# Two gated chunks in the plain form instead of four, twenty from seven products, in the second feed-forward layer

## The chip, the cores and the metric

The kernel runs on one core of a Trainium2 chip. The metric is the device time of one execution in microseconds (us), from the first instruction to the last with what the launch adds around them; lower is better.

## The reference, cut to what matters

A decoder trunk of two layers over 1024 tokens of width 1024: a Conformer convolution layer, then a differential-attention layer, each followed by a SwiGLU feed-forward layer with 2816 hidden units, and a last RMSNorm. The change touches only the second feed-forward layer:

```python
def swiglu(h, w1, w3, w2):
    return (jax.nn.silu(h @ w1) * (h @ w3)) @ w2

x = x + swiglu(rmsnorm(x, ffn_norm_g[layer]), ffn_w1[layer], ffn_w3[layer], ffn_w2[layer])
```

## The kernel before, in words

All activations stand transposed: 128 channels on the partitions, 1024 tokens in two halves LA and LB of 512. Every float32 product is made from three fp32r matmuls: each operand is split into a high part (a rounded copy, made by ScalarE) and a low part (the difference, made by VectorE), and high by low, low by high and high by high are added up in PSUM. The function `product` issues these three; one of them has a 128x128 weight tile and 512 columns.

The 2816 hidden units are 22 chunks of 128. For the gated part of the second layer (`silu(h @ w1) * (h @ w3)`) there are two forms.

**The plain form.** `F1` holds its plan; its `sizes` say how many chunks are made so. A chunk has two blocks, one of w1 and one of w3. A block is 8 chunks of the contraction, 3 matmuls and 2 halves: 48 matmuls, issued by `both` (line 2160), and the last block by `dense` (lines 2022 to 2024). Blocks are numbered i = 0, 1, ... On each block VectorE and ScalarE do, in order: split the weights of block i + 2 (`hi`, line 923; `lo`, line 1367), then what the function `beside_f1(i)` holds, then the evacuation. A w1 block is evacuated by a multiplication with `rstd` (line 1561, semaphore `t1_ok`) and a Silu (line 1049); a w3 block by two VectorE operations for each half (lines 1572 and 1575, `t3_ok` and `g_ok`). The gated rows go to DRAM (`hidden_store`).

**Seven products (Winograd's form of Strassen's method).** The other chunks are taken in pairs. A unit is one matrix (w1 or w3) for a pair of chunks: the weights and the operand are each four quarters, and seven products (`A11, S2, A12, S1, S3, S4, A22`) of sums of quarters replace eight. A product is 4 chunks of the contraction and 3 matmuls: 12 matmuls, so a unit is 84. `UNITS = FC - CHUNKS0`, which is 18 units for the 18 chunks. The sums of the operand's quarters are made once, before the first unit, by this chain:

- ScalarE `sum_parts` (line 1274, 8 copies) makes `tv`; VectorE `sums_first` (lines 1834 and 1837, 4 + 4 operations) and `sums_last` (lines 1843 and 1846, 4 + 4) make the sums in `tv`.
- ScalarE `sum_high` (line 1281) makes the high part of a sum, VectorE `sum_low(n, turn)` (line 1853) its low part, 4 operations each for each of the sums 1, 3, 2 and at last 0. Sum 0 lies over an operand of the plain form, and so its `sum_high` waits until the last plain block is done.
- For unit 0, the weights' sums: `weight_sums_first` and `weight_sums_last` (lines 1877 to 1887, 4 operations), and the splits of six products' weights, `up_high` (line 1297) and `up_low` (line 1862). The seventh, `A22`, comes after the last plain block.

All of these VectorE operations have 512 columns. In the kernel before they stand beside blocks 2 to 7, as the diff shows. TensorE waits before each product for that product's `up_low` (`u_lo`), in unit 0 also for the `sum_low` of its operand, and for the PSUM bank. Every engine works through its instructions strictly in the order written.

The weights of unit 0 are loaded by `up_load(0)`, which SyncE issues behind the `hidden_store` of an earlier chunk and after the last `lo`; `up_load(u + 1)` waits for all seven `up_low` of unit u. Behind the last unit the down projection begins (`STEPS_D` steps in three parts of tokens); `DOWN_ORDER` names the order in which part 0 uses the banks, which follows from the bank of the last product.

Of the kernel before, what the change touches and what calls it, by code (L numbers as in the profile page):

```python
# [18 lines left out]
KC = D // P  # L19
TB = T // P  # L20
F = 2816
FC = F // P
# [13 lines left out]
LA, LB = 0, 1  # L36
# [64 lines left out]
F0B = Ffn(0, (LB,), (8, 7, 7), PW2B + KC, F0A.result0 + F0A.results() + KC, FC, 0, 3 * KC, False)  # L101
ATT0 = F0B.block0 + F0B.blocks()
WO0 = ATT0 + 3 * HEADS
F1 = Ffn(1, (LA, LB), (4,), WO0 + KC + 1, F0B.result0 + F0B.results(), 2 * FC, FC, 6 * KC, False, True)
TAIL = F1.block0 + F1.blocks()
BLOCKS = TAIL

CHUNKS0 = F1.sizes[0]  # L110
UNITS = FC - CHUNKS0
# [9 lines left out]


PARTS = ((0, HT), (HT, HT // 2), (HT + HT // 2, HT // 2))
DOWN_ORDER = ((2, 3, 6, 7, 4, 5, 0, 1), tuple(range(KC)), tuple(range(KC)))
DOWN_BANK = (tuple((n, 0) for n in range(KC)), tuple(((2, 3, 6, 7)[n // 2], n % 2 * HT // 2) for n in range(KC)),
             tuple(((4, 5, 0, 1)[n // 2], n % 2 * HT // 2) for n in range(KC)))
STEPS_D = len(PARTS) * FC
# [36 lines left out]
def results_through(b):  # L164
# [9 lines left out]
    if b < ATT0:  # L174
        return F0B.result0 + b - F0B.block0 + 1
    return F1.result0 + 2 * (b - F1.block0 + 1)

# [184 lines left out]
def trunk(nc, a, out):  # L362
    with ExitStack() as ctx:
# [5 lines left out]
        def sem(name):  # L369
            return ctx.enter_context(nc.semaphore(name))  # L370
# [157 lines left out]
        t1_ok = sem("t1_ok")  # L528
        t3_ok = sem("t3_ok")
# [86 lines left out]
        def down_size(b):  # L616

            for f in (F0A, F0B, F1):
                if f.block0 <= b < f.block0 + f.blocks():
# [24 lines left out]
        def _(sp):  # L644
# [19 lines left out]
            def cols(w, n):  # L664
                return w[:, :, n * P:(n + 1) * P]
# [20 lines left out]

            up1 = w1[F1.layer].rearrange("(k p) n -> p k n", p=P)
            up3 = w3[F1.layer].rearrange("(k p) n -> p k n", p=P)
            down = w2[F1.layer].rearrange("(k p) (n c) -> k p n c", p=P, c=P)
# [45 lines left out]
            def second_layer():  # L735
                blocks = list(F1.order())
                for _, what, c, b in blocks[0:4]:
                    load(b, cols(up1 if what == "w1" else up3, c))
                for i in range(len(blocks)):
                    if i + 4 < len(blocks):  # L740
                        _, what, c, b = blocks[i + 4]
                        load(b, cols(up1 if what == "w1" else up3, c))
                    if i == 6:
                        up_load(0)
                    if i % 2:
                        hidden_store(i // 2)
                for u in range(UNITS):
                    if u + 1 < UNITS:
                        up_load(u + 1)
                    else:  # L750
                        down_load(0)
                        down_load(1)
                    if u % 2:
                        for j in range(4):
                            if u == UNITS - 1 and j == 3:
                                down_load(2)
                                down_load(3)
                            unit_store(u, j)
                            if u == UNITS - 1 and j < 2:
                                hidden_load(2 * j)  # L760
                                hidden_load(2 * j + 1)
                for d in range(4, STEPS_D):
                    down_load(d)
                    hidden_load(d)
                    if d == 8:
                        for j in range(4):
                            sp.wait_ge(g_out[j], 16 * (UNITS // 2))
                        sp.dma_start(grow[:, :], a["final_norm_g"].unsqueeze(0).broadcast_to([P, D])) \
                            .then_inc(grow_in, 16)
                    t = y_behind(d - 8)  # L770
                    if t is not None:
                        y_store(t)
# [111 lines left out]
        def _(act):  # L884
# [385 lines left out]
            def sum_parts():  # L1270

                for k in range(HC):
                    for to, hf in ((tv[1], LA), (tv[2], LB)):
                        act.activation(by_block(to[:, k, :]), X(k, hf), ACT.Copy,
                                       scale=col("ffn_norm_g", KC + k)).then_inc(t_e, 1)
# [25 lines left out]
                act.activation(st[:, j, :], st[:, j, :], ACT.Silu).then_inc(u_silu, 1)  # L1301

            def beside_f1(i):
                if i == 2:
                    sum_parts()
                if i == 4:
                    sum_high(1, HC)
                if i == 5:
                    sum_high(3, 2 * HC)
                    sum_high(2, 3 * HC)  # L1310
                if i == 7:
                    for j in range(A22):
                        up_high(0, j)

# [45 lines left out]
        def _(dve):  # L1360
# [469 lines left out]
            def sums_first():  # L1830

                for k in range(HC):
                    dve.wait_ge(t_e, 2 * k + 2)
                    dve.tensor_tensor(tv[0][:, k, :], tv[2][:, k, :], tv[1][:, k, :], ALU.subtract).then_inc(t_v, 1)
                for k in range(HC):
                    dve.wait_ge(t_v, k + 1)
                    dve.scalar_tensor_tensor(by_block(tv[1][:, k, :]), X(HC + k, LB), col("ffn_norm_g", KC + HC + k),
                                             by_block(tv[0][:, k, :]), ALU.mult, ALU.subtract).then_inc(t_v, 1)

            def sums_last():  # L1840
                for k in range(HC):
                    dve.wait_ge(t_v, HC + k + 1)
                    dve.scalar_tensor_tensor(by_block(tv[3][:, k, :]), X(HC + k, LA), col("ffn_norm_g", KC + HC + k),
                                             by_block(tv[1][:, k, :]), ALU.mult, ALU.subtract).then_inc(t_v, 1)
                for k in range(HC):
                    dve.scalar_tensor_tensor(by_block(tv[2][:, k, :]), X(HC + k, LB), col("ffn_norm_g", KC + HC + k),
                                             by_block(tv[2][:, k, :]), ALU.mult, ALU.subtract).then_inc(t_v, 1)

            def sum_low(n, turn):

                for k in range(HC):
                    dve.wait_ge(t_hi, HC * turn + k + 1)
                    dve.tensor_tensor(Tl[n][:, k, :], tv[n][:, k, :], Th[n][:, k, :].bitcast(F32),
                                      ALU.subtract).then_inc(t_lo, 1)
# [32 lines left out]
                dve.tensor_tensor(s4, raw[0][:, HC:KC, :], s2v[:, :, :], ALU.subtract).then_inc(u_sum, 1)  # L1887

            def beside_f1(i):
                if i == 3:  # L1890
                    sums_first()
                if i == 4:
                    sums_last()
                if i == 5:
                    sum_low(1, 0)
                if i == 6:
                    sum_low(3, 1)
                    sum_low(2, 2)
                if i == 7:
                    weight_sums_first(0)  # L1900
                    weight_sums_last(0)
                    for j in range(A22):
                        up_low(0, j)
# [66 lines left out]
            def down_adds(part):  # L1970

                t0, w = PARTS[part]
                for i, n in enumerate(DOWN_ORDER[part]):
                    bank, c0 = DOWN_BANK[part][n]
# [28 lines left out]
        def _(pe):  # L2003
# [416 lines left out]
            def up_product(u, j):  # L2420
                q = PRODUCTS * u + j
                pe.wait_ge(u_lo, q + 1)
                if u == 0 and j in sums_of:
                    pe.wait_ge(t_lo, HC * sums_of[j])
                if q >= len(UBANKS):
                    product_read(q - len(UBANKS))
                elif q < 2:
                    pe.wait_ge(std_ok, 8)
                elif q < 4:
                    pe.wait_ge(t3_ok, F1.plain(0, CHUNKS0 - 2, 1) + 1)  # L2430
                elif q < 6:
                    pe.wait_ge(t1_ok, F1.plain(0, CHUNKS0 - 1, 1) + 1)
                else:
                    pe.wait_ge(t3_ok, F1.plain(0, CHUNKS0 - 1, 1) + 1)
                h, l = quarters[j]
                r = uslot(q)
                for k in range(HC):
                    ins = product(ps[:, ubank(q), :], Uh[r][:, k, :], Ul[r][:, k, :], h[:, k, :], l[:, k, :], k == 0,
                                  k == HC - 1)
                ins.then_inc(up_mm, 1)  # L2440
# [5 lines left out]
            def down_free(part, n):  # L2446

                bank = DOWN_BANK[part][n][0]
                if part == 0:
                    product_read(ALL_PRODUCTS - KC + DOWN_ORDER[0].index(n))  # L2450
                elif part == 1:
                    pe.wait_ge(dx_ok, DOWN_ORDER[0].index(bank) + 1)
                else:
# [13 lines left out]
            for d in range(STEPS_D):  # L2467
# [5 lines left out]

                for n in DOWN_ORDER[part]:
                    bank, c0 = DOWN_BANK[part][n]
# [37 lines left out]
```

## Time and profile before

| | |
|---|---|
| median of 3 runs | 2335.47 us (2334.7 to 2335.96) |
| the profiled execution, its own time | 2335.3 us |
| its span | 2333.5 us |
| mean granted TensorE clock | 0.995 |
| TensorE matmul busy | 2283.1 us, 98% |
| VectorE busy | 1614.2 us, 69% |
| ScalarE busy | 905.8 us, 39% |
| plain blocks of the second layer | from 1639.37 to 1728.27 us of the span |
| 18 units of seven products | from 1728.27 to 2071 us of the span |

The profile is of one execution. Busy times are of each engine; 1.8 us of that execution's time lie outside the span. In the rows, PE is TensorE's matmul, PEld its weight load, DVE is VectorE, ACT is ScalarE, SPq is the queue of DMA issues of SyncE. A matmul's own duration is longer than the distance to the next, since they are pipelined: the starts tell the rate.

### The profile page before, as it was taken

To read this page: it belongs to the slowest core of one execution; us is meant where nothing else is said; L and a number is where in the kernel's file an instruction comes from. 1 tells how busy PE (TensorE), PEld (TensorE's weight loads), DVE (VectorE), ACT (ScalarE), POOL (GpSimd) and SP (SyncE) were. 2 spreads that over 40 slices of the span, in tenths; PEclk is the share of its full clock that TensorE was granted. 3 is DMA by queue.
4 is the path that set the end of the run, shared out by engine and by line. 5 is a ranking of instruction groups with operands and counts; after the bars stand their busy time and mean duration, and the time that the engine had idled before them with its cause. 6 is when DMAs were issued, how large, how long until landed. Compare 5 with 4: busy or idle time off the path is not lost.

```text
span 2333.5 us, 28680 instructions
## 1 busy us (share of the span) xinstructions
PE 2283.1 (98%) x11177; PEld 1875.9 (80%) x11177; DVE 1614.2 (69%) x2487; ACT 905.8 (39%) x1571; POOL 67.9 (3%) x51
## 2 busy tenths in 40 slices
PE   7999989999999999999999999999999999999998
PEld 6885768888888888887777777787788888888898
DVE  6998589989566634445677777774878887863465
ACT  5221532222344422233455555663532323232354
POOL 0000000000000000002111111000000000000000
PEclk9999999999999999999999999999999999999999
DMA  4110223323333333322111111211112222264574
GB/s 138 49 37 18 73 72 99 100 86 97 93 95 99 91 99 95 104 86 77 37 37 37 37 37 37 68 52 54 55 54 86 77 86 77 86 209 140 160 249 158
DMA packets 280324, 200.88 MB, mean 86 GB/s; under 512 B 7973, under 2 KB 258686, under 8 KB 280190
## 3 DMA queue, kind: packets, MB, share of 16 engines
q1 hardware_dynamic: 280190, 199.04, 28.0%
q8 instruction: 90, 1.47, 0.3%
q14 instruction: 44, 0.36, 0.0%
HBM read 180.14 MB, written 18.87 MB: 85 GB/s over the span
## 4 chain that ended last, share of the span: by engine, by line
PE 89%; DVE 8%; ACT 1%; issue 1%; SPq 0%; DMA 0%; DVEq 0%; ACTq 0%
PE ps L2022 28%; PE ps L2024 27%; PE ps L2023 27%; PE ps L2160 3%; PE ps L2005 3%; DVE cacc L1442 2%; DVE cvA L1442 2%; PE ps L2118 1%; DVE sc L1693 1%; ACT sc L1136 1%; PE ps L2077 0%; DVE Wl L1367 0%; DVE Sl L1608 0%; PE ps L2087 0%; DVE rstd L1380 0%
## 5 line engine op out<-in xcount | busy, mean ns | idle before, releaser
L2022 PE MATMUL ps<-Sh,Wl 128*128 128x512 f32 x1616 | 655.6, 406 | 16.3 <-DVE Sl L1530 7.1
L2024 PE MATMUL ps<-Sh,Wh 128*128 128x512 f32 x1616 | 632.5, 391 | 0.0
L2023 PE MATMUL ps<-Sl,Wh 128*128 128x512 f32 x1616 | 631.5, 391 | 0.0
L2022 PEld LDWEIGHTS ps<-Sh,Wl 128*128 128x128 f32 x1616 | 305.0, 189 | 94.5 <-issue 33.0
L2024 PEld LDWEIGHTS ps<-Sh,Wh 128*128 128x128 f32 x1616 | 304.4, 188 | 65.7
L2023 PEld LDWEIGHTS ps<-Sl,Wh 128*128 128x128 f32 x1616 | 305.3, 189 | 59.7 <-issue 3.4
L1367 DVE TENSOR_TENSOR Wl<-raw,Wh 128x1024 fp32r<-128x1024 f32 (+1 forms) x178 | 213.3, 1198 | 87.4 <-ACT Wh L923 86.1
L923 ACT ACTIVATE Wh<-raw 128x1024 fp32r<-128x1024 f32 (+1 forms) x178 | 183.2, 1032 | 152.6 <-DMA raw<-in_ffn_w_dram 126.1
L2022 PE MATMUL ps<-Dh,Wl 128*128 128x256 f32 (+1 forms) x528 | 168.6, 319 | 1.5 <-DVE Wl L1929 1.5
L2024 PE MATMUL ps<-Dh,Wh 128*128 128x256 f32 (+1 forms) x528 | 168.1, 318 | 0.0
L2023 PE MATMUL ps<-Dl,Wh 128*128 128x256 f32 (+1 forms) x528 | 168.0, 318 | 0.0
L2022 PE MATMUL ps<-G0h,Wl 128*128 128x512 f32 x352 | 138.6, 394 | 0.0
L2024 PE MATMUL ps<-G0h,Wh 128*128 128x512 f32 x352 | 137.0, 389 | 0.0
L2023 PE MATMUL ps<-G0l,Wh 128*128 128x512 f32 x352 | 137.0, 389 | 0.0
L1149 ACT ACTIVATE ATh<-ps 128x512 fp32r<-128x512 f32 (+2 forms) x96 | 47.1, 491 | 187.4 <-PE ps L2005 187.4
L1707 DVE TENSOR_TENSOR ATl<-ps,ATh 128x512 fp32r<-128x512 f32 (+2 forms) x96 | 53.3, 556 | 88.2 <-ACT ATh L1149 88.2
L2022 PE MATMUL ps<-Sh,Ul 128*128 128x512 f32 x288 | 112.0, 389 | 0.0
L2023 PE MATMUL ps<-Sl,Uh 128*128 128x512 f32 x288 | 112.0, 389 | 0.0
L2024 PE MATMUL ps<-Sh,Uh 128*128 128x512 f32 x288 | 112.0, 389 | 0.0
L1052 ACT ACTIVATE G0h<-tmp 128x512 fp32r<-128x512 f32 x44 | 27.8, 633 | 209.4 <-DVE tmp L1565 117.3
L2022 PEld LDWEIGHTS ps<-Dh,Wl 128*128 128x128 f32 x528 | 100.6, 190 | 8.8 <-DVE Wl L1929 1.9
L2023 PEld LDWEIGHTS ps<-Dl,Wh 128*128 128x128 f32 x528 | 100.6, 190 | 6.9
(260 smaller groups left out, 3912.6 us busy)
## 6 DMA issues: line engine op xcount, KB each, us to landing
raw<-in_ffn_w_dram SPq DMA_DIRECT2D x182, 512.0 KB, 3.9
raw<-in_pw_w_dram SPq DMA_DIRECT2D x32, 512.0 KB, 3.9
draw<-in_ffn_w_dram SPq DMA_DIRECT2D x32, 512.0 KB, 4.2
raw<-in_ffn_w_dram SPq DMA_DIRECT2D x32, 448.0 KB, 3.7
g_dram<-st SPq DMA_DIRECT2D x36, 256.0 KB, 2.1
graw<-g_dram SPq DMA_DIRECT2D x22, 256.0 KB, 3.7
graw<-g_dram SPq DMA_DIRECT2D x44, 128.0 KB, 4.3
xrow<-in_x_dram SPq DMA_DIRECT2D x8, 512.0 KB, 6.8
```

The source lines that it names most:

```text
L923: act.activation(flat(ring_hi(b)), flat(raw[b % 2][:, 0:n, :]), ACT.Copy).then_inc(w_hi, 1)
L1052: act.activation(G0h[:, c, :], tmp[:, 2 + c % 2, :], ACT.Copy).then_inc(hid_hi, 1)
L1136: act.activation(v, v, ACT.Exp, bias=negmax[:, m:m + 1], scale=-1.0, accum_out=rowsum[:, m:m + 1]).then_inc(e_ok, 1)
L1149: act.activation(ATh[:, j0:j0 + nj, (i % 2) * P:(i % 2 + 1) * P], ps[:, BANK[key], 0:nj * P].rearrange("p (j q) -> p j q", q=P), ACT.Copy) ...
L1367: dve.tensor_tensor(flat(ring_lo(b)), flat(raw[b % 2][:, 0:n, :]), flat(ring_hi(b)).bitcast(F32), ALU.subtract).then_inc(w_lo, 1)
L1442: dve.scalar_tensor_tensor(dst, src, wj, dst, ALU.mult, ALU.add).then_inc(conv_s, 1)
L1707: dve.tensor_tensor(ATl[:, j0:j0 + nj, qs], ps[:, BANK[key], 0:nj * P].rearrange("p (j q) -> p j q", q=P), ATh[:, j0:j0 + nj, qs].bitcast( ...
L2005: return pe.transpose(dst, src, ident[0:m, 0:m])
L2022: pe.matmul(dst, ll, rh, start=start, stop=False)
L2023: pe.matmul(dst, lh, rl, start=False, stop=False)
L2024: return pe.matmul(dst, lh, rh, start=False, stop=stop)
L2160: ins = pe.matmul(ps[:, banks[j], :], (Wh if m else Wl)[s][:, k, :], l if m == 1 else h, start=k == 0 and m == 0, stop=k == chunks - 1 and ...
```

## The change

`F1.sizes` goes from 4 to 2, so `CHUNKS0` is 2, there are 4 plain blocks, and 20 units. `beside_f1` of ScalarE and of VectorE, which laid the chain of the sums beside blocks 2 to 7, now lays it beside blocks 1 to 3. The banks from which the first products are freed, and `DOWN_ORDER`, follow the new counts. `up_load(0)` stands at i == 2 rather than 6, in both cases two blocks ahead of the first unit.

```diff
-F1 = Ffn(1, (LA, LB), (4,), WO0 + KC + 1, F0B.result0 + F0B.results(), 2 * FC, FC, 6 * KC, False, True)
+F1 = Ffn(1, (LA, LB), (2,), WO0 + KC + 1, F0B.result0 + F0B.results(), 2 * FC, FC, 6 * KC, False, True)
...
-DOWN_ORDER = ((2, 3, 6, 7, 4, 5, 0, 1), tuple(range(KC)), tuple(range(KC)))
+DOWN_ORDER = ((0, 1, 2, 3, 6, 7, 4, 5), tuple(range(KC)), tuple(range(KC)))
...
-                    if i == 6:
+                    if i == 2:
                         up_load(0)
...
             def beside_f1(i):          # ScalarE
+                if i == 1:
+                    sum_parts()
                 if i == 2:
-                    sum_parts()
-                if i == 4:
                     sum_high(1, HC)
-                if i == 5:
+                if i == 3:
                     sum_high(3, 2 * HC)
                     sum_high(2, 3 * HC)
-                if i == 7:
                     for j in range(A22):
                         up_high(0, j)
...
             def beside_f1(i):          # VectorE
+                if i == 1:
+                    sums_first()
+                if i == 2:
+                    sums_last()
+                    sum_low(1, 0)
                 if i == 3:
-                    sums_first()
-                if i == 4:
-                    sums_last()
-                if i == 5:
-                    sum_low(1, 0)
-                if i == 6:
                     sum_low(3, 1)
                     sum_low(2, 2)
-                if i == 7:
                     weight_sums_first(0)
                     weight_sums_last(0)
                     for j in range(A22):
...
                 elif q < 4:
+                    pe.wait_ge(t1_ok, F1.plain(0, CHUNKS0 - 1, 1) + 1)
+                elif q < 6:
+                    pe.wait_ge(t3_ok, F1.plain(0, CHUNKS0 - 1, 1) + 1)
+                else:
                     pe.wait_ge(t3_ok, F1.plain(0, CHUNKS0 - 2, 1) + 1)
-                elif q < 6:
-                    pe.wait_ge(t1_ok, F1.plain(0, CHUNKS0 - 1, 1) + 1)
-                else:
-                    pe.wait_ge(t3_ok, F1.plain(0, CHUNKS0 - 1, 1) + 1)
```

## Rows read from the trace of the kernel before

**Rows 1.** The page, part 1: busy us, share of the span, instructions.

```profile
PE 2283.1 (98%) x11177; PEld 1875.9 (80%) x11177; DVE 1614.2 (69%) x2487; ACT 905.8 (39%) x1571; POOL 67.9 (3%) x51
```

**Rows 2.** Busy time by stage: the 18 units; then PEclk, DMA share, GB/s.

```profile
1730.00:2071.00 341.00, 341.00 (x1506) 282.14 (x1504) 272.95 (x424) 104.65 (x180) 0.00 (x0) 1.00 0.29 86
```

**Rows 3.** Timeline, TensorE: start us, us, line, tiles, count, idle before.

```profile
1684.74 0.62 PE L2160 MATMUL ps<-Sh,Wl 128*128 128x512 f32 x2
...
1728.27 0.39 PE L2022 MATMUL ps<-Sh,Ul 128*128 128x512 f32 x1
...
2070.76 0.39 PE L2024 MATMUL ps<-T4h,Uh 128*128 128x512 f32 x1
2072.61 0.47 PE L2022 MATMUL ps<-Dh,Wl 128*128 128x512 f32 x1 [1.46 <-DVE Wl L1929]
```

**Rows 4.** Timeline, VectorE, plain blocks to the start of the units.

```profile
1669.50 1.29 DVE L1561 TENSOR_TENSOR tmp<-ps,rstd 128x512 f32<-128x512 f32 x2
1672.44 1.23 DVE L1367 TENSOR_TENSOR Wl<-raw,Wh 128x1024 fp32r<-128x1024 f32 x1 [1.65 <-ACT Wh L923]
...
1683.85 2.73 DVE L1837 SCALAR_TENSOR_TENSOR tv<-xT,vec,tv 128x512 f32<-128x512 f32 x4
1686.50 0.68 DVE L1572 TENSOR_TENSOR tmp<-ps,rstd 128x512 f32<-128x512 f32 x1
...
1689.15 1.22 DVE L1367 TENSOR_TENSOR Wl<-raw,Wh 128x1024 fp32r<-128x1024 f32 x1
1690.29 2.73 DVE L1843 SCALAR_TENSOR_TENSOR tv<-xT,vec,tv 128x512 f32<-128x512 f32 x4
...
1695.60 1.29 DVE L1561 TENSOR_TENSOR tmp<-ps,rstd 128x512 f32<-128x512 f32 x2
...
1709.14 2.49 DVE L1853 TENSOR_TENSOR T4l<-tv,T4h 128x512 fp32r<-128x512 f32 x4
1711.55 2.49 DVE L1853 TENSOR_TENSOR T3l<-tv,T3h 128x512 fp32r<-128x512 f32 x4
1717.36 1.29 DVE L1561 TENSOR_TENSOR tmp<-ps,rstd 128x512 f32<-128x512 f32 x2 [3.32 <-PE ps L2160]
1718.57 0.68 DVE L1877 TENSOR_TENSOR Us<-raw 128x512 f32<-128x512 f32 x1
...
1721.09 0.69 DVE L1862 TENSOR_TENSOR Ul<-raw,Uh 128x512 fp32r<-128x512 f32 x1
```

**Rows 5.** Timeline, ScalarE, the same stretch.

```profile
1671.36 1.99 ACT L923 ACTIVATE Wh<-raw 128x1024 fp32r<-128x1024 f32 x2
1673.26 5.00 ACT L1274 ACTIVATE tv<-xT,vec 128x512 f32<-128x512 f32 x8
...
1696.32 1.23 ACT L1049 ACTIVATE tmp<-tmp 128x512 f32<-128x512 f32 x2 [9.08 <-DVE tmp L1561]
1697.46 1.04 ACT L923 ACTIVATE Wh<-raw 128x1024 fp32r<-128x1024 f32 x1
1698.41 2.18 ACT L1281 ACTIVATE T4h<-tv 128x512 fp32r<-128x512 f32 x4
```

**Rows 6.** Timeline, TensorE, after its two longest stops in the first layer.

```profile
245.97 0.77 PE L2022 MATMUL ps<-Sh,Wl 128*128 128x512 f32 x1 [4.37 <-DVE upB L1416]
...
251.23 0.49 PE L2022 MATMUL ps<-Sh,Wl 128*128 128x512 f32 x1
...
307.98 0.76 PE L2022 MATMUL ps<-Sh,Wl 128*128 128x512 f32 x1 [6.85 <-DVE Sl L1530]
...
313.08 0.39 PE L2022 MATMUL ps<-Sh,Wl 128*128 128x512 f32 x1
```

**Rows 7.** Windows around the first of them: us, PE busy (count), PEclk, DMA, GB/s.

```profile
246.00:251.30 5.30, 5.30 (x13) 0.50 0.02 5
```

**Rows 8.** SyncE's issues on line 698, all units: us from issue to landing.

```profile
DMA to landing us min/median/max: 3.9/5.2/6.2
```

**Rows 9.** Timeline, VectorE, end of part 0 of the down projection.

```profile
2189.76 4.87 DVE L1977 TENSOR_TENSOR xT<-ps,xT 128x512 f32<-128x512 f32 x8
```

## The prediction, as it went on record

> **What bounds the kernel now.** I read the page first: TensorE is busy for 98% of the span [rows 1], so the first guess is that any matmul taken out is time won. That share is a mean over stages, so the windows by stage come next. In the units of seven products TensorE never pauses (341.00 of 341 us), and VectorE is at 272.95 us, 80% [rows 2]: both matter there, TensorE leads. Then the timeline of TensorE at the seams of the stage: unit 0 starts at 1728.27 us on the heels of the last plain block, and the last matmul of unit 17 starts at 2070.76 [rows 3]. 18 units are 1512 matmuls, so the step between two is (2070.76 - 1728.27) / 1511 = 226.7 ns. A unit takes 84 x 0.2267 = 19.04 us, a plain block 48 x 0.2267 = 10.88 us.
>
> The timeline of VectorE ahead of unit 0 is the view that decides. The first `up_low` starts at 1721.09 [rows 4], only 7.2 us before TensorE reaches unit 0. On the way VectorE paused for TensorE, 3.32 us before 1717.36. So VectorE is ahead by a few us in the kernel before, and it gets there because it has six blocks in which to make the sums. VectorE is late at the beginning of the layer: its first evacuation (of block 0) starts at 1669.50 [rows 4], when TensorE has two blocks behind it and is well inside the third. Before that VectorE makes squares, their sums and the reciprocals of `rstd`; the change touches none of it.
>
> **TensorE's work.** Two chunks in the plain form are 4 blocks, 192 matmuls. From seven products they are 2 units, 168 matmuls. The change takes 24 matmuls out: 24 x 0.2267 = 5.44 us. This is all that TensorE has to win. (The Trainium skill, "TensorE: Matmul & The Clock Gate", section "Back-to-back issue gap", gives about 131 ns as the spacing of a sustained stream at 512 columns; by that estimate the saving were 24 x 0.131 = 3.1 us. The trace does not agree, it has 226.7 ns.)
>
> **What is moved.** TensorE now needs the first product's weights after block 3, not 7. In the trace block 4 starts at 1684.74 [rows 3]; that is when unit 0 could start. Nothing ahead of it changes: blocks 0 to 3, their weights and the banks are as before. TensorE gets there 43.5 us earlier (four blocks). VectorE is spared only what belongs to the four blocks: 4 `lo` by 1.14 us, which is the distance from 1689.15 to 1690.29, two evacuations of w1 at 1.21 and two of w3 at 2.65 (from 1686.50 to 1689.15), 12.3 us in all, and its pauses for TensorE. The sums, 32 operations for the operand and the weights, stay. So I walk VectorE's queue in its new order, with the distances of [rows 4, 5]:
>
> 1. Up to the last `lo`, start 1672.44, nothing changes. ScalarE then has one weight split fewer ahead of `sum_parts` (0.95 us of the 1.99), so that starts at 1672.3 rather than 1673.26; its 8 copies take 5.00 us.
> 2. `sums_first`: the four differences each need two of those copies, so they run at ScalarE's pace. The last copy ends at 1677.3, the last difference starts at 1677.4, the next operation at 1678.0. The four of line 1837 take 2.65 (from 1683.85 to 1686.50): 1680.6.
> 3. Evacuation of block 1, 2.65: 1683.3.
> 4. `sums_last`, 5.31 (from 1690.29 to 1695.60): 1688.6. `sum_low(1, 0)`, 2.41 (from 1709.14 to 1711.55): 1691.0. Its high parts are long made.
> 5. Evacuation of block 2 starts at 1691.0. ScalarE needs it for the Silu and stands before its `sum_high(3)` until then. From the start of line 1561 (1695.60) to where ScalarE is free after the Silu (1697.46) it is 1.86 us, so the high part starts at 1692.9 and the first is there at 1693.5. VectorE is free at 1692.2 and pauses for 1.3 us: a new wait.
> 6. `sum_low(3)` and `sum_low(2)`, 8 x 0.603 (a quarter of that 2.41) = 4.8: 1698.4. The weights of unit 0 are in by then: `up_load(0)` goes out after the gated rows of block 1, about 1683.5, and the slowest load of that line landed after 6.2 us [rows 8].
> 7. The weights' sums, 2.52 (from 1718.57 to 1721.09): 1700.9. The first `up_low` takes 0.69, and TensorE starts 0.1 later: 1701.7.
>
> TensorE stands still from 1684.74 to 1701.7: 17.0 us. The second to the sixth `up_low` follow at 0.6 us each, faster than products are consumed (2.72 us each), so the wait is paid once.
>
> VectorE's spacing bears all of this. The Trainium skill, "VectorE: DVE Perf Modes", section "The DRAIN you can't avoid", says that a next operation doesn't start until the pipe has emptied, and its section on the errata gives 691 ns for a float32 sum of two tensors at 512 columns. By this estimate the chain's some 40 operations at 0.69 rather than 0.603 would end 3.5 us later, for a stall of 20.5 us. The durations in the trace agree (0.68 to 0.69), but the starts are 0.60 apart where nothing holds the next one.
>
> **The clock.** The rows hold two places where TensorE resumes after a stop of some us [rows 6]. After each of them it runs at the lower of its two levels, 1.2 GHz: the granted clock from 246.0 to 251.3 is 0.50 [rows 7]. From 245.97 to 251.23 it starts 12 matmuls in 5.26 us, from 307.98 to 313.08 12 in 5.10 us. At full clock 12 take 2.72 us, so a restart costs 2.54 or 2.38 us. A stop of 17 us is longer than both, so I take 2.45 us. Below, it could be nothing, if the clock should come back at once; above, twice that, if it drops again in unit 0.
>
> **Is anything late next?** Product 3 (`S1`) needs the low part of sum 0, which VectorE makes behind six `up_low` (to 1704.5) and the evacuation of block 3 (2.65) in 2.41 us: ready at 1709.6. TensorE reaches product 3 at 1701.7 + 2.45 + 3 x 2.72 = 1712.3 (1709.9 at full clock). It fits, by 2.7 or 0.3 us. Unit 1: its load waits for `A22`'s `up_low` at 1710.1 and lands by 1716.3 at the slowest [rows 8], the two first sums and the first `up_low` take 1.9 us, so 1718.2 against TensorE's 1723.2: 5 us of room. Later units repeat the pattern of the kernel before. SyncE issues two stores fewer for each plain chunk and more for the units; neither queue is near its limit. `DOWN_ORDER`: part 1 now starts with bank 2 when three additions are done, not one. They start at 2189.76, 0.60 apart, so the third is done at 2191.7, and TensorE comes to part 1 at 2072.61 + 22 x 24 x 0.2267 = 2192.3 [rows 3, 9]. Cover 0.6 us, cost nothing; without it, it would be at most 1.2 us.
>
> **The sum.** -5.44 + 17.0 + 2.45 = +14.0 us. The profiled execution took 2335.3 us (span 2333.5), 0.2 below the median. Predicted time 2335.3 + 14.0 = 2349.3 us, 0.6% slower.
>
> **The rivals.**
> - *The sums are hidden and the 24 matmuls are won* (the other side): 2335.3 - 5.4 = 2329.9 us. For it speaks that VectorE is busy for only 69% of the span, against it the walk above. It decides if `up_low` is through before 1684.74, 17 us ahead of where I have it; break-even, with the restart paid, would be 1687.7. The step that could be wrong by this much is where VectorE begins: if its 1669.50 came earlier. Nothing in the diff moves that. 3%.
> - *The stop costs no clock*: 2335.3 - 5.4 + 17.0 = 2346.9 us. Against it are both restarts in the rows. 7%.
> - *A second wait in units 0 and 1*: sum 0, the load of unit 1 or a second drop of the clock, each 1 to 3 us: 2351 to 2353 us. The room of product 3 is small only at full clock. 13%.
> - *The walk is a little off*, since the pause of step 5 (1.3 us) or that for ScalarE in step 2 (about 1.3) goes away, or both: 1 to 3 us less stall, 2346.3 to 2348.3. 10%.
> - *VectorE's starts are as far apart as its operations last* (0.69 us, from the rows of single operations, not 0.603): some 40 operations by 0.087 us are 3.5 us more of stall, 2352.8 us. Against it is every group of four in rows 4. 2%. The rule of the Trainium skill named above would bring this about.
>
> **How the numbers follow.** The likeliest case, 2348.3 to 2350.6, has 65%. The range 2345.5 to 2352.5 takes in the cases without the clock's price and with a smaller stall, down to part of both together, and most of the second wait. A difference of 0.2% (4.7 us) is about what a measurement of this kernel can tell from no change. Faster 0.03, within it 0.01, slower 0.96.
>
> **What would show it.** TensorE idle for some 17 us ahead of the first matmul on `Uh`, the releaser `Ul` L1862 (in the new file's line); VectorE without a pause for TensorE from its first evacuation to the units, only some 1.3 us for ScalarE; a granted clock of 0.50 for some 5 us after the restart, and 12 matmuls in about 5.2 us; then 20 units of 19.04 us without idle. The prediction is wrong if the stop is absent or under 5 us, if a second stop appears in units 0 to 2, or if the down projection starts with more than its 1.46 us.

## The result, and the profile after

| | kernel before | changed kernel |
|---|---|---|
| median of 4 executions, us | 2335.46 (2334.7 to 2335.96) | 2352.33 (2347.7 to 2352.77) |
| ratio, 95% interval | | 1.0068 [1.0056, 1.0080] |
| profiled execution, us | 2335.3 | 2347.7 |
| its span, us | 2333.5 | 2345.9 |

The changed kernel is 0.7% slower. In the new file the lines of the trace stand one to three lower: `up_low` is L1861, the matmuls are L2019 to L2021. The profiled execution is the fastest of the four, 4.5 us below the next one; a second profile of the same kernel (e1, below) has a span of 2348.7, and both are read in what follows.

The page, part 1, of the changed kernel (answers to [rows 1]):

```profile
PE 2276.5 (97%) x11153; PEld 1869.6 (80%) x11153; DVE 1634.0 (70%) x2519; ACT 910.3 (39%) x1583; POOL 67.9 (3%) x51
```

There are 24 matmuls fewer, as the diff says; TensorE is busy for 6.6 us less and the span is 12.4 us longer. This part of the page doesn't say where. The waits of TensorE in the second layer's up projection do (what waited, what for, us in total, times, longest):

```profile
PE ps L2019 <- DVE Ul L1861: 17.6, 3, 16.6
PE ps L2019 <- DVE Wl L1926: 1.7, 1, 1.7
```

In the kernel before only the second stood there, with 1.5 us. Now there is one long wait for `Ul`, and two short ones that were not forecast. TensorE's timeline places them (changed kernel; answers to [rows 3]):

```profile
1682.19 0.39 PE L2021 MATMUL ps<-Sh,Wh 128*128 128x512 f32 x1
1699.22 0.80 PE L2019 MATMUL ps<-Sh,Ul 128*128 128x512 f32 x1 [16.65 <-DVE Ul L1861]
...
1703.40 0.40 PE L2019 MATMUL ps<-T2h,Ul 128*128 128x512 f32 x1
...
2025.06 0.50 PE L2019 MATMUL ps<-Sh,Ul 128*128 128x512 f32 x1 [0.51 <-DVE Ul L1861]
...
2063.88 0.50 PE L2019 MATMUL ps<-Sh,Ul 128*128 128x512 f32 x1 [0.44 <-DVE Ul L1861]
...
2082.83 0.39 PE L2021 MATMUL ps<-T4h,Uh 128*128 128x512 f32 x1
2084.92 0.47 PE L2019 MATMUL ps<-Dh,Wl 128*128 128x512 f32 x1 [1.70 <-DVE Wl L1926]
```

The next matmul was due at 1682.19 + 0.23 and came at 1699.22: a stop of 16.80 us. The 12 matmuls of product 1 then take 1703.40 - 1699.22 = 4.18 us where 2.72 is their full pace. The short waits stand at the head of units 17 and 19.

VectorE's timeline in the same stretch (changed kernel; answers to [rows 4]):

```profile
1667.17 1.29 DVE L1560 TENSOR_TENSOR tmp<-ps,rstd 128x512 f32<-128x512 f32 x2
...
1675.01 0.69 DVE L1833 TENSOR_TENSOR tv<-tv,tv 128x512 f32<-128x512 f32 x1 [0.53 <-ACT tv L1274]
1675.62 2.73 DVE L1836 SCALAR_TENSOR_TENSOR tv<-xT,vec,tv 128x512 f32<-128x512 f32 x4
1678.27 0.68 DVE L1571 TENSOR_TENSOR tmp<-ps,rstd 128x512 f32<-128x512 f32 x1
...
1680.92 2.73 DVE L1842 SCALAR_TENSOR_TENSOR tv<-xT,vec,tv 128x512 f32<-128x512 f32 x4
...
1686.23 2.48 DVE L1852 TENSOR_TENSOR T2l<-tv,T2h 128x512 fp32r<-128x512 f32 x4
1688.64 1.27 DVE L1560 TENSOR_TENSOR tmp<-ps,rstd 128x512 f32<-128x512 f32 x2
1691.13 2.50 DVE L1852 TENSOR_TENSOR T4l<-tv,T4h 128x512 fp32r<-128x512 f32 x4 [1.21 <-ACT T4h L1281]
1693.54 2.49 DVE L1852 TENSOR_TENSOR T3l<-tv,T3h 128x512 fp32r<-128x512 f32 x4
1695.95 0.68 DVE L1876 TENSOR_TENSOR Us<-raw 128x512 f32<-128x512 f32 x1
...
1698.48 0.69 DVE L1861 TENSOR_TENSOR Ul<-raw,Uh 128x512 fp32r<-128x512 f32 x1
```

This execution reaches the stage 2.33 us sooner than the profile before (first evacuation 1667.17, not 1669.50). That lead was gained in the first layer, which the change doesn't touch (TensorE is back from its first long stop there at 242.84 us, not at 245.97 as in [rows 6]), and it is not in e1's profile, so it is no effect of the change; what brought it is not shown. With 2.33 taken off, the walk of the prediction falls on these starts within 0.15 us: 1680.6 is 1678.27, 1683.3 is 1680.92, 1688.6 is 1686.23, 1691.0 is 1688.64, 1693.5 is 1691.13, 1698.4 is 1695.95 (0.12 off), 1700.9 is 1698.48, and TensorE's 1701.7 is 1699.22 (0.15 off). The pause for ScalarE was forecast at 1.3 us and is 1.21.

A window gives sums over a stretch of time. These are the two behind the stop (changed kernel; us, then busy time of PE, PEld, DVE, ACT, POOL with counts, PEclk, DMA share, GB/s; they answer [rows 7]):

```profile
1699.20:1702.00 2.80, 2.78 (x7) 2.22 (x8) 2.80 (x5) 2.80 (x6) 0.00 (x0) 0.50 0.00 0
1702.00:1704.00 2.00, 2.00 (x10) 1.65 (x9) 1.97 (x4) 0.71 (x2) 0.00 (x0) 0.98 0.00 0
```

The clock was at its lower level, 1.2 GHz, for 2.8 us here and not for the 5 us of [rows 7].

### The profile page after: what moved, and what is told of

Same layout as the page of the kernel before. It is cut to its first block, busy times and chain, and to the rows that moved or that the text cites. A ratio compares the mean times of both kernels' runs of the same rounds, so it can differ in the third digit from the quotient of the medians.

```text
span 2345.9 us, 28704 instructions
## 1 busy us (share of the span) xinstructions
PE 2276.5 (97%) x11153; PEld 1869.6 (80%) x11153; DVE 1634.0 (70%) x2519; ACT 910.3 (39%) x1583; POOL 67.9 (3%) x51
## 4 chain that ended last, share of the span: by engine, by line
PE 81%; DVE 13%; issue 2%; DMA 2%; ACT 2%; SPq 0%; DVEq 0%; ACTq 0%
PE ps L2019 26%; PE ps L2021 25%; PE ps L2020 25%; PE ps L2002 3%; DMA raw<-in_ffn_w_dram 2%; DVE cacc L1441 2%; DVE Ul L1861 2%; DVE cvA L1441 2%; PE ps L2115 1%; PE ps L2157 1%; DVE sc L1692 1%; ACT sc L1136 1%; DVE rstd L1379 0%; DVE va L1917 0%; DVE Wl L1366 0%
## 5 line engine op out<-in xcount | busy, mean ns | idle before, releaser
L2019 PE MATMUL ps<-Sh,Wl 128*128 128x512 f32 x1616 | 655.6, 406 | 16.7 <-DVE Sl L1529 7.1
L2021 PE MATMUL ps<-Sh,Wh 128*128 128x512 f32 x1616 | 632.3, 391 | 0.0
L2019 PEld LDWEIGHTS ps<-Sh,Wl 128*128 128x128 f32 x1616 | 305.0, 189 | 95.0 <-issue 33.2
L2021 PEld LDWEIGHTS ps<-Sh,Wh 128*128 128x128 f32 x1616 | 304.4, 188 | 65.7
L1366 DVE TENSOR_TENSOR Wl<-raw,Wh 128x1024 fp32r<-128x1024 f32 (+1 forms) x174 | 208.4, 1198 | 84.0 <-ACT Wh L923 82.9
L2019 PE MATMUL ps<-Dh,Wl 128*128 128x256 f32 (+1 forms) x528 | 168.6, 319 | 1.7 <-DVE Wl L1926 1.7
L2021 PE MATMUL ps<-Dh,Wh 128*128 128x256 f32 (+1 forms) x528 | 168.1, 318 | 0.0
L2019 PE MATMUL ps<-Sh,Ul 128*128 128x512 f32 x320 | 125.5, 392 | 17.6 <-DVE Ul L1861 17.6
L2019 PE MATMUL ps<-G0h,Wl 128*128 128x512 f32 x352 | 138.6, 394 | 0.0
L2021 PE MATMUL ps<-G0h,Wh 128*128 128x512 f32 x352 | 137.0, 389 | 0.0
L2021 PE MATMUL ps<-Sh,Uh 128*128 128x512 f32 x320 | 125.0, 391 | 0.0
L2020 PE MATMUL ps<-Sl,Uh 128*128 128x512 f32 x320 | 125.0, 391 | 0.0
L2019 PEld LDWEIGHTS ps<-Dh,Wl 128*128 128x128 f32 x528 | 100.6, 190 | 9.0 <-DVE Wl L1926 2.1
L2021 PEld LDWEIGHTS ps<-Dh,Wh 128*128 128x128 f32 x528 | 100.6, 190 | 6.9
```

What stands on the lines that cost most here:

```text
L1366: dve.tensor_tensor(flat(ring_lo(b)), flat(raw[b % 2][:, 0:n, :]), flat(ring_hi(b)).bitcast(F32), ALU.subtract).then_inc(w_lo, 1)
L2019: pe.matmul(dst, ll, rh, start=start, stop=False)
L2020: pe.matmul(dst, lh, rl, start=False, stop=False)
L2021: return pe.matmul(dst, lh, rh, start=False, stop=stop)
```

## The experiments

The theory, after the result: VectorE's queue alone decides when TensorE starts on unit 0 (stop of 17 us); the restart at the lower clock costs 1.5 to 2.5 us; four blocks less cover and nothing else is the reason. Rivals: the load of unit 0 decides; the restart costs nothing and the time went elsewhere; there is a second loss in the units.

### e1: the changed kernel once more

No edit.

> The changed kernel, unaltered, for more executions and a second profile. Its four executions so far were 2347.7 (profiled) and 2352.2 to 2352.8 us, so 4.6 us apart. Theory A (the early stage): the profiled one was lucky in the first layer, where it reached VectorE's first evacuation of the plain blocks at 1667.17 us against 1669.50 before, and in the restart (1.46 us dearer than at full clock, not 2.45). Then another profile shows about 1669.5 us there, a restart of about 2.4 us, and 2351 to 2352 us. Theory B (the units): the stop and the start are the same in every execution and the 20 units differ, since VectorE's lead is gone and each wait for a load of weights stops TensorE; then the units take some 4 us more than 20 x 19.04 = 380.8 us in a profile of 2352 us.

Measured: 2351.68 us (2350.72 to 2352.06), ratio 1.0068 [1.0053, 1.0083]; span 2348.7. The stop is 16.81 us, product 1 takes 4.64 us. TensorE's timeline and two windows (e1):

```profile
1701.85 0.80 PE L2019 MATMUL ps<-Sh,Ul 128*128 128x512 f32 x1 [16.66 <-DVE Ul L1861]
```

```profile
1701.80:1704.00 2.20, 2.15 (x5) 1.76 (x6) 2.20 (x4) 2.20 (x5) 0.00 (x0) 0.50 0.00 0
1704.00:1706.00 2.00, 2.00 (x6) 1.56 (x6) 1.97 (x4) 1.33 (x3) 0.00 (x0) 0.56 0.00 0
```

The stop repeats to 0.01 us, the lower clock does not: it lasts about 4 us here. Theory A holds in the main: the early stage is back at 1669.79 us and the median is 2351.68, though the restart costs 1.92 us and not 2.4. Theory B is out: the units take 1.3 us more than their pure pace, not 4. With e1's span and that of the changed kernel's first profile, each against 2333.5, the terms add up as follows. "Units" is the time from product 2 of unit 0 to the last matmul of unit 19, less 1667 steps of 0.22667 us (the prediction's 226.7 ns with one more digit); "before down" is the step to the down projection, against that in [rows 3].

| term, us | forecast | first profile | e1 |
|---|---|---|---|
| up to the first evacuation | 0 | -2.33 | +0.29 |
| 24 matmuls less | -5.44 | -5.44 | -5.44 |
| stop before unit 0 | +17.0 | +16.80 | +16.81 |
| product 1 at the lower clock | +2.45 | +1.46 | +1.92 |
| units | 0 | +1.57 | +1.30 |
| before down | 0 | +0.24 | +0.25 |
| down projection to the end | 0 | +0.09 | +0.06 |
| sum | +14.0 | +12.39 | +15.19 |
| difference of the spans | | 12.4 | 15.2 |

### e2: two of the four sums of the operand left out

```diff
-                    sum_high(3, 2 * HC)
-                    sum_high(2, 3 * HC)
...
-                    sums_last()
                     sum_low(1, 0)
...
-                    sum_low(3, 1)
-                    sum_low(2, 2)
...
-                        S3: (Th[2], Tl[2]), A22: (Th[3], Tl[3])}
+                        S3: (Sh[:, LA, 0:HC], Sl[:, LA, 0:HC]), A22: (Sh[:, LA, HC:KC], Sl[:, LA, HC:KC])}
```

It leaves out the two sums for `S3` and `A22`; these products read plain quarters of the operand, so as many matmuls run.

> Leaves out two of the four sums of the operand (VectorE's sums_last, 8 operations, and the low parts of sums 3 and 2, 8 operations, with ScalarE's 8 high parts); products S3 and A22 read plain quarters in their place, so their results are not the reference's. Theory (VectorE's queue sets the end of the stop): the chain is shorter by 5.31 + 4.82 + 1.2 for the pause behind the Silu = 11.3 us, the stop falls from 16.65 to 5.3 us, and the time by 11 us against the changed kernel, about 2341 us, a little less if the restart is cheaper. Rival (the load of unit 0 or ScalarE sets it): the stop stays over 10 us and the time above 2346 us.

Measured: 2343.00 us (2342.18 to 2344.36), ratio 1.0032 [1.0021, 1.0044]; span 2342.0. VectorE has 16 operations (5.3 and 4.8 us) and the pause of 1.2 us less ahead of the first `up_low`, 11.3 us. The stop falls from 16.8 to 8.2, by 8.6 and not 11.3. TensorE's, VectorE's, ScalarE's and SyncE's timelines (e2):

```profile
1693.22 0.80 PE L2014 MATMUL ps<-Sh,Ul 128*128 128x512 f32 x1 [8.01 <-DVE Ul L1859]
```

```profile
1689.94 0.69 DVE L1874 TENSOR_TENSOR Us<-raw 128x512 f32<-128x512 f32 x1 [2.68 <-issue]
```

```profile
1689.93 0.63 ACT L1297 ACTIVATE Uh<-raw 128x512 fp32r<-128x512 f32 x1 [2.01 <-DMA raw<-in_ffn_w_dram]
```

```profile
1682.36 1.67 SPq L705 DMA_DIRECT2D g_dram<-tmp  x2
1684.07 1.16 SPq L698 DMA_DIRECT2D raw<-in_ffn_w_dram  x2
```

VectorE now stands for 2.68 us ahead of the weights' sums: the load of unit 0 (L698) goes out at 1684.07, behind the store of chunk 0 (L705), and ScalarE's first operation on it starts at 1689.93, released by the DMA. So VectorE's queue is what bounds the changed kernel, and the load of unit 0 is the next bound, 8.6 us earlier. Both theories have a part, one after the other; the stop of 16.8 us is VectorE's. The time came out 2 us above the forecast 2341: the stop kept 2.9 us more than forecast, and TensorE has three more short waits, at units 13, 17 and 19, 2.3 us together. The units lose 3.4 us here, 2.1 more than in e1.

### e3: TensorE kept busy in the stop

```diff
+            pe.wait_ge(std_ok, 8)
+            for _ in range(70):
+                pe.matmul(ps[:, 6, :], Sh[:, LA, 1, 0:P], Sh[:, LA, 0, :], start=True, stop=True)
             for u in range(UNITS):
```

The added matmuls write to a bank that the next product overwrites.

> The changed kernel with 70 matmuls of 512 columns put on TensorE in the stop, into a bank that is overwritten afterwards; they add nothing to the result. 70 x 0.2267 = 15.9 us of the 16.65. Theory (the restart runs at the lower clock for some us): the granted clock stays at 1.00, the first 12 matmuls of unit 0 take 2.72 us, and the time falls by 1.5 to 2.5 us against the changed kernel. Rival (the clock costs nothing): no difference beyond 0.5 us.

Measured: 2348.74 us (2346.55 to 2349.33), ratio 1.0054 [1.0038, 1.0071]; span 2346.4. TensorE's timeline and a window (e3):

```profile
1684.74 16.03 PE L2441 MATMUL ps<-Sh 128*128 128x512 f32 x70
1701.58 0.50 PE L2019 MATMUL ps<-Sh,Ul 128*128 128x512 f32 x1 [0.81 <-DVE Ul L1861]
```

```profile
1701.50:1704.00 2.50, 2.42 (x10) 1.99 (x11) 2.50 (x6) 2.50 (x6) 0.00 (x0) 1.00 0.00 0
```

Unit 0 starts at 1701.6, within 0.3 us of e1's 1701.85, but the clock is at its full level, and product 1 takes 2.89 us, not 4.64. The median is 2.9 us below e1's, more than the 1.5 to 2.5 forecast; of the 2.3 us between the two profiled spans 1.75 are product 1. The restart has a price of its own; it is not part of the stop. (The Trainium skill, "TensorE: Matmul & The Clock Gate", section "What's actually happening", says that the throttled clock is the default and activity releases it, and that how many matmuls run slowly at a kernel's start differs from run to run of one kernel. The traces here agree, for a restart inside a kernel: the granted clock behind the stop is 0.50 and then 1.00 again, with the fillers it is 1.00 throughout, and the same 12 matmuls are 1.46 us dearer than at full clock in the first profile of the changed kernel and 1.92 in the second.)

### e4: the change in the other direction, six plain chunks

```diff
-F1 = Ffn(1, (LA, LB), (4,), WO0 + KC + 1, F0B.result0 + F0B.results(), 2 * FC, FC, 6 * KC, False, True)
+F1 = Ffn(1, (LA, LB), (6,), WO0 + KC + 1, F0B.result0 + F0B.results(), 2 * FC, FC, 6 * KC, False, True)
...
-DOWN_ORDER = ((2, 3, 6, 7, 4, 5, 0, 1), tuple(range(KC)), tuple(range(KC)))
+DOWN_ORDER = ((6, 7, 4, 5, 0, 1, 2, 3), tuple(range(KC)), tuple(range(KC)))
```

Against the kernel before; the sums and the load of unit 0 stand beside the last six of twelve blocks.

> Six chunks in the plain form, 16 units, the sums again beside the six blocks ahead of the last. Theory (two chunks in the plain form are 24 matmuls dearer and nothing else waits): the kernel of before plus 5.4 us, 2340.9 us, with TensorE never idle between the plain blocks and the last unit. Rival (TensorE's pace in the units is not its own but VectorE's or the loads'): less than 4 us or more than 7 us.

Measured: 2342.45 us (2339.84 to 2343.26), ratio 1.0029 [1.0019, 1.0039]; span 2341.0. TensorE's waits and timeline, then VectorE's (e4):

```profile
PE ps L2022 <- DVE xT L1977: 1.6, 1, 1.6
PE ps L2022 <- DVE Wl L1929: 1.5, 1, 1.5
```

```profile
1771.65 0.39 PE L2024 MATMUL ps<-Sh,Wh 128*128 128x512 f32 x1
1771.88 0.39 PE L2022 MATMUL ps<-Sh,Ul 128*128 128x512 f32 x1
...
2199.75 0.36 PE L2022 MATMUL ps<-Dh,Wl 128*128 128x256 f32 x1 [1.65 <-DVE xT L1977]
```

```profile
2195.33 4.87 DVE L1977 TENSOR_TENSOR xT<-ps,xT 128x512 f32<-128x512 f32 x8
```

Up to the down projection all is as the theory counted: no idle before unit 0 or in the units, and 24 matmuls more are 5.44 us. The median is 7.1 us above that of before, not 5.4: inside what the rival allowed, but not for its reason, since the pace in the units is TensorE's own. What comes on top is a wait of 1.65 us that the prediction had named as possible for the changed kernel: part 1 of the down projection begins with bank 2, which this order puts seventh among the additions of L1977. 5.44 + 2.0 (down projection to the end, 262.86 against 260.89 us) + 0.1 is 7.5, the difference of the spans. Both neighbours of the kernel before, with two and with six plain chunks, are slower than it.

### e5: `A22`'s low part before the last evacuation of a unit

```diff
                     up_low(u + 1, S4)
+                    up_low(u + 1, A22)
...
                 result_of(u, 3, A22, E_21, q6, LA)
-                if more:
-                    up_low(u + 1, A22)
```

Against the changed kernel. It asks what the two short waits in the units are. The chain there is a ring: the load of unit u + 1 waits for `A22`'s `up_low`, the sums wait for the load, the low parts for the sums. Units 16 and 17 of the changed kernel, VectorE, then SyncE:

```profile
2016.33 0.68 DVE L1861 TENSOR_TENSOR Ul<-raw,Uh 128x512 fp32r<-128x512 f32 x1
...
2022.98 0.69 DVE L1876 TENSOR_TENSOR Us<-raw 128x512 f32<-128x512 f32 x1 [3.91 <-DMA raw<-in_ffn_w_dram]
```

```profile
2017.04 1.14 SPq L698 DMA_DIRECT2D raw<-in_ffn_w_dram  x2
```

And the first sum of unit 3 and of unit 19 (changed kernel, VectorE):

```profile
1752.77 0.69 DVE L1876 TENSOR_TENSOR Us<-raw 128x512 f32<-128x512 f32 x1 [4.11 <-DMA raw<-in_ffn_w_dram]
...
2061.80 0.69 DVE L1876 TENSOR_TENSOR Us<-raw 128x512 f32<-128x512 f32 x1 [4.33 <-DMA raw<-in_ffn_w_dram]
```

The lead is the time from a unit's first sum to its first matmul. 16 units in 309.03 us are 19.31 us each on average, TensorE needs 19.04: a unit costs 0.27 us of the lead. It does not go evenly. In every unit the load goes out 0.03 us behind `A22`'s split, and the first sum on it starts 5.7 to 6.7 us after that; the lead falls where the load is one of the slow ones. The first sums are also by turns some 18.0 and 20.3 us apart, so the odd units have the smaller leads: 5.05 us at unit 3, 3.21 at unit 9, 2.77 at unit 15, 2.08 at units 17 and 19, which are the two that TensorE waits for. In the kernel before it is the same (1739.48 to 2048.72 for 16 units, 19.33), but there VectorE is 7.3 us ahead at unit 3, here 5.0, and there are two units fewer: there the last first sum comes 3.2 us ahead of TensorE, here 2.1, which is too little.

> The changed kernel with VectorE's up_low of A22 of the next unit one step earlier, ahead of the read of product A22 (2 or 3 operations, 1.4 to 2.0 us), so that the load of the unit after it goes out sooner. Theory (load, sums, splits and back to the load are a ring that takes a little longer than TensorE's 19.04 us a unit, and after the change it starts without a lead): the two waits of 0.2 to 0.5 us late in the units are gone, the pause of VectorE for the load falls below 2 us in each unit, and the time falls by 1 to 2.5 us, to 2349.5 to 2351 us. Rival (what the median has above the forecast lies elsewhere): no difference beyond 0.5 us.

Measured: 2349.99 us (2348.02 to 2350.90), ratio 1.0061 [1.0046, 1.0076]; span 2348.9. TensorE's waits, and VectorE's group of first sums between 1730 and 2071 us (e5; count, busy, mean ns, idle before it and its releaser):

```profile
PE ps L2018 <- DVE Ul L1861: 16.7, 1, 16.7
PE ps L2018 <- DVE Wl L1926: 1.5, 1, 1.5
```

```profile
L1876 DVE TENSOR_TENSOR Us<-raw 128x512 f32<-128x512 f32 x18 | 12.4, 691 | 27.2 <-DMA raw<-in_ffn_w_dram 27.1
```

The short waits are gone, the wait before the down projection is 1.5 again, and VectorE's idle time for the loads is 27 us, not the 56.6 of the changed kernel in the same stretch. The pause did not fall below 2 us in each unit, as forecast: it is at most 0.8 us in the even units from unit 2 on, and still 2.4 to 3.7 in the odd ones from unit 3 on. The units take 0.4 us more than their pure pace, where the changed kernel has 1.57 and 1.30, and nearly all of the 0.4 is the end of the restart, whose lower clock reaches into product 2 here. The mechanism is shown by the rows. That the median gains by it, 1.7 us below e1's, is not: the two sets of times overlap, and this profile lost at the restart (2.57 us in product 1) and ahead of the stage (0.99) what it won.

### e6: the sums early, the number of chunks as before

```diff
+                if i == 1:
+                    sum_parts()
                 if i == 2:
-                    sum_parts()
-                if i == 4:
                     sum_high(1, HC)
-                if i == 5:
+                if i == 3:
...
+                if i == 1:
+                    sums_first()
+                if i == 2:
+                    sums_last()
+                    sum_low(1, 0)
                 if i == 3:
-                    sums_first()
-                if i == 4:
-                    sums_last()
-                if i == 5:
-                    sum_low(1, 0)
-                if i == 6:
                     sum_low(3, 1)
                     sum_low(2, 2)
```

Against the kernel before, with eight plain blocks; the sums of unit 0's weights stay beside block 7.

> Four plain chunks as before, but the operand's sums beside blocks 1 to 3 as in the change; the weights of unit 0 stay beside the last block. Theory (moving the sums costs nothing while four more blocks cover VectorE): the time of the kernel before within 1 us, TensorE waits at most 0.5 us for a weight split of a plain block. Rival (the early sums delay the evacuations and the weight splits of the plain blocks): TensorE stops between blocks 3 and 6 for several us.

Measured: 2336.31 us (2334.06 to 2337.81), ratio 1.0006 [0.9996, 1.0015]; span 2335.2. TensorE's waits in the second layer's up projection (e6):

```profile
PE ps L2021 <- DVE Wl L1928: 1.5, 1, 1.5
PE ps L2159 <- DVE Wl L1367: 0.5, 1, 0.5
```

Putting the same operations beside the early blocks costs 0.5 us of waiting, and the median is within 1 us of the kernel before, as forecast; the interval takes in no difference at all. The place of the sums is not what costs 17 us; that no blocks stand behind them is.

### e7: the sums in the order in which products need them

```diff
-                    if i == 2:
+                    if i == 0:
                         up_load(0)
...
-                if i == 1:
+                if i == 2:
                     sums_first()
-                if i == 2:
-                    sums_last()
+                    weight_sums_first(0)
+                    up_low(0, A11)
+                    sums_third()
                     sum_low(1, 0)
+                    up_low(0, S2)
                 if i == 3:
-                    sum_low(3, 1)
-                    sum_low(2, 2)
-                    weight_sums_first(0)
-                    weight_sums_last(0)
-                    for j in range(A22):
-                        up_low(0, j)
+                    up_low(0, A12)
+                    up_low(0, S1)
+                    sum_low(0, 1)
...
-            sum_low(0, 3)
+            sums_second()
+            sum_low(2, 2)
+            weight_sums_last(0)
+            up_low(0, S3)
+            up_low(0, S4)
+            sum_low(3, 3)
             up_low(0, A22)
```

Against the changed kernel. `sums_third` and `sums_second` are the halves of `sums_last`; ScalarE's high parts are put in the same order, and the load of unit 0 is issued beside block 0.

> The changed kernel with the chain in the order in which the products need it: the load of unit 0 ahead of the first store; after the evacuation of block 1 the sums for product S2 only, the splits of A11, S2, A12 and S1, then the other two sums, between the first products. Same operations, same number. Theory (VectorE's queue bounds, so its order decides when TensorE can start): unit 0 starts within 1 us of the end of block 3; then shorter stops ahead of S2 (about 1.4 us), S3 (about 6) and unit 1 (about 3), 10 to 12 us in all rather than 16.8 + 1.9, and about 2344 to 2346 us. Still slower than before. Rival (the total of VectorE's work counts, whatever its order): the stops add up to 17 us again and the time stays at 2351 us.

Measured: 2347.67 us (2346.33 to 2350.03), ratio 1.0055 [1.0038, 1.0071]; span 2345.3. TensorE's timeline (e7):

```profile
1685.23 0.39 PE L2026 MATMUL ps<-Sh,Ul 128*128 128x512 f32 x1
...
1689.51 0.50 PE L2026 MATMUL ps<-T2h,Ul 128*128 128x512 f32 x1 [1.40 <-DVE Ul L1864]
...
1704.13 0.80 PE L2026 MATMUL ps<-T3h,Ul 128*128 128x512 f32 x1 [6.13 <-DVE Ul L1864]
...
1715.46 0.50 PE L2026 MATMUL ps<-Sh,Ul 128*128 128x512 f32 x1 [1.47 <-DVE Ul L1864]
...
1947.55 0.50 PE L2026 MATMUL ps<-Sh,Ul 128*128 128x512 f32 x1 [1.14 <-DVE Ul L1864]
```

Unit 0 now starts on the heels of block 3, with no stop. The wait comes back in pieces, ahead of `S2`, `S3` and unit 1: 9.0 us in place of 16.65. Then the ring bites sooner: five more waits between 1869 and 2064 us, 2.4 us together. The first sum comes 2.07 to 2.08 us ahead of TensorE at every odd unit from unit 1 on, so here the ring sets the pace all along, 19.33 us a unit between units 3 and 19. From the start of unit 1 to the last matmul that costs 5.3 us (366.80 us, where 1595 steps at full pace are 361.54), more than the rows name as waits. Neither theory nor rival foresaw this: the stop is cut up and shorter, as the theory says, but the time is 1.7 us above the forecast 2344 to 2346.

### e8: e7 with e5's edit

Its diff is that of e7 and that of e5.

> e7 and e5 together. Theory: both gains add up, 1 to 2 us under e7; the kernel before stays the fastest. Rival: a time under 2335 us, if the stops of e7 are smaller than worked out.

Measured: 2341.85 us (2338.05 to 2343.78), ratio 1.0026 [1.0014, 1.0038]; span 2339.8. TensorE's waits from unit 0 to the down projection (e8):

```profile
PE ps L2025 <- DVE Ul L1864: 9.2, 3, 6.1
PE ps L2025 <- DVE Wl L1928: 1.5, 1, 1.5
```

The first three waits stay (9.2 us), the later ones are gone. The median is 5.8 us below e7's, and every execution is below every one of e7. That is far more than the 1 to 2 us forecast, since the edit of e5 is worth more where the ring sets the pace all along: from the start of unit 1 to the last matmul e8 takes 361.68 us, 0.1 above full pace, where e7 loses 5.3. This pair is what shows the ring in the times, and not only in the rows. It is the fastest of the versions with two plain chunks that were run, and it is still slower than the kernel before: the 5.44 us of the matmuls stand against 9.2 us of waiting and the restart behind the stop of 6.1, which costs about 1.5 us: the three products from `S3` on, 36 matmuls, take 9.7 us in place of 8.16.

## Why the prediction was right

2349.3 us were forecast, 2352.33 measured, inside the range and on the right side; the size of the loss was 3 us too small. The median lies 0.17 us under the upper end of the range, outside of the likeliest case (2348.3 to 2350.6), in the band that was priced for a second wait in units 0 and 1, which did not come. So the mechanism that carries the forecast, a stop of 17 us and a dear restart, was right, and that the number is still in the range owes something to luck. By the prediction's own steps:

- **TensorE's work**, -5.44 us: right. e4 measures the same 24 matmuls with the other sign and finds them whole.
- **The walk of VectorE's queue**, steps 1 to 7: right to 0.15 us at each of its stations, and the stop was 16.8 us, not 17.0. The rival that VectorE's starts are 0.69 us apart is out by it, and so is the one that the walk is 1 to 3 us off. (The Trainium skill, "VectorE: DVE Perf Modes", section "The DRAIN you can't avoid", which the prediction sets against the trace, goes on to say that a next operation that is not held starts earlier; read to its end it agrees with the 0.60 us between starts.) e2 shows that VectorE's queue and not the load decides, and that the load of unit 0 would be next after 8.6 us.
- **The clock**, +2.45 us: the mechanism was right (e3 takes it away), the term was too large for the changed kernel's two profiles, 1.46 and 1.92 us, and a little small for e5's, 2.57. The two restarts in the rows of before were two draws, and the price varies by more than they showed.
- **Is anything late next?** For units 0 and 1 it was right: no second wait there. For "Later units repeat the pattern of the kernel before" it was wrong, and this is the step that failed. It compared places in the pattern and not pace: a unit takes VectorE's ring 19.31 us on average against TensorE's 19.04. That was to be read in the trace of before, where the first sums of 16 units lie 19.33 apart. A lead of 7.3 us at unit 3 bears it for 18 units, one of 5.0 not for 20. e5 takes the waits away, and e7 and e8 show the price with a smaller lead. It cost 1.3 to 1.6 us in the units, and 0.24 before the down projection, whose wait was 1.7 in place of 1.5 us. The prediction had looked for a second wait in units 0 to 2; it came in units 17 and 19. One of its own signs of being wrong did appear, the down projection that starts with more than 1.46 us of waiting.
- **`DOWN_ORDER`**: right for the change, no wait in the traces. e4 shows that the step is no empty worry: 1.65 us, with bank 2 seventh.
- **Not settled.** In the profile of e1 the terms add up to 15.2 us, while its median lies 16.4 above that of before. The executions without a profile are about 1 us above the profiled one there, and 4.5 to 5.1 us above it in the first four. No run has a trace of such an execution, so where this time goes stays open.

## What to carry to other kernels

When work is moved under fewer blocks, walk the queue of the engine that does it, start by start, from its last fixed point; a busy share of 70% says nothing about whether it is through in time. Then compare the pace of each ring (load, sums, splits, slot free again) with the pace of the engine that it feeds: a lead that shrinks by 0.27 us a unit on average is harmless until it starts smaller or has to last longer. A stop costs more than its length, since the clock comes back later than the work.

## What was not expected of the hardware

The price of a restart is not a constant. After the same stop of 16.8 us, to 0.01, the 12 matmuls of product 1 took 4.18, 4.64 and 5.29 us in three profiles (the changed kernel, e1, e5), with the granted clock at 0.50 for some 3, 4 and 6 us. After e7's stop of 6.1 us the granted clock was 0.50 as well, in the window 1702:1706 us, and 0.71 in the next two. In e5 it was 0.50 from 1702.55 to 1708.5 us, past the end of product 1.

And in e5 the load of the odd units did not follow `A22`'s split, though it waits for nothing else of VectorE's. Against the start of unit 17 on TensorE (2025.06 in the changed kernel, 2029.19 in e5) the split starts 15.9 us ahead and not 8.7, which is 7.1 us sooner, but the load goes out 12.7 us ahead and not 8.0, only 4.7 sooner. The stores of the unit before, each of which waits for its evacuation, are ahead of it in SyncE's queue and end at 2016.43 (e5, SyncE):

```profile
2008.26 8.16 SPq L710 DMA_DIRECT2D g_dram<-st  x3
2016.47 1.19 SPq L698 DMA_DIRECT2D raw<-in_ffn_w_dram  x2
```
